# The down product of the second feed-forward as seven block products per chunk

## The chip, the cores and the metric

The kernel runs on one core of one Trainium2 chip. The metric is the device time of one launch in microseconds, the median of the runs shown. One execution of it was also recorded by the hardware profiler. The engines are named as the profile names them: PE multiplies matrices (PEld loads its weights beside it), DVE is the vector engine, ACT the scalar engine, POOL the GpSimd engine, and SP issues the transfers.

## The reference, cut to what matters

The program is a block with a gated linear attention mixer and a feed-forward, and a second block with a hybrid mixer and another feed-forward. The change is in the last stage, the second feed-forward, over 1024 tokens and a model width of 1024, in float32:

```
D_FF = 4 * D_MODEL                                   # 4096
h = rms_norm(x, norm_mlp[l])
x = x + jnp.square(jax.nn.relu(h @ w_up[l])) @ w_down[l]
return rms_norm(x, norm_final)
```

## The kernel before

**Precision.** Every float32 product is made of three matmuls. Each operand is split into a high part (ACT copies it to the shorter type, `Ring.high`) and a low part (POOL subtracts the high part from the whole, `Ring.low`; for activations it is DVE). The three are high by high, high by low, low by high.

**Stage.** `square_ffn` walks over D_FF in 16 chunks of 256 columns. A chunk i has an *up* part (`up(i)`), whose 256 by 1024 result (columns of D_FF by tokens) is made as seven block products named P1, P5, P7, P6, P2, P4, P3 by `PRODUCTS`, in four PSUM banks (tiles PA and PB). Each of the seven has 12 matmuls of 128x512. Sums of the four weight blocks are needed for it, and POOL makes four of them per chunk (`pair_low`, into S, which the profile calls f_sums, and over a block of the raw weights). Before them POOL multiplies the two raw weight tiles by the norm's weights (`weigh`, 128x1024 each). DVE joins the results (`combine`, five adds), ACT applies relu, and DVE multiplies relu by the value (`prod`) for the square.

The *down* part of chunk i takes the activations of up(i-1), 256 by 1024, and the matching 256 rows of w_down. It has 16 output tiles of 128 tokens by 512 columns, in the four PSUM banks of DD and MM in turn, each with 2 times 3 matmuls. DVE adds each tile to X (`add`, 128x512) and raises `down_add`; PE waits for it before it writes a bank again. That is 84 up matmuls and 96 down matmuls in a chunk, and 11 split weight blocks (7 up, 4 down).

**Order.** PE does up(0), and then up(i), down(i) for i = 1 to 15, and then the down part of the last 256 rows (chunk 16) together with the final norm, tile by tile. Everything is written out by hand: each engine runs its own list in order and waits on semaphores. The split weight blocks go through a ring of six slots (`views`, `free`): ACT may write a slot's high part only when PE has used what was there (`used`). `split` counts the low parts that POOL has made, `hi_done` the high parts. SP loads the raw weights: the up tiles of the next chunk when POOL has made all but one of this chunk's low parts (`load_pair`), the down rows into slots of their own (`load_down`), 256 KB each.

**ACT's list in a chunk** (`rest` and the loop): three weight highs, the two activation highs (`a_high`, 128x1024), three weight highs, `keep` (a copy of one bank), one high, four down highs, and relu of both banks.

**DVE's list in a chunk**: `combine`, 16 times `add` with `prod` after the first two, then `a_low` twice (128x1024, both inputs in SBUF). PE waits for `a_lo` only once per chunk, ahead of its first down tile.

## Time and profile before

| | us |
|---|---|
| median of 3 runs | 2822.59 |
| lowest and highest | 2822.29, 2824.02 |
| span of the profiled execution | 2819.2 |

The span is what the profiler saw from the first to the last instruction; it is 3.4 us under the median. The last stage starts on PE at 2154.25 us of the span, and its 15 chunks with an up and a down part follow each other from 2174.99 us on. In the profile, a timeline has one line per instruction with its start and its duration in us; `x2` is two of them merged, and brackets tell how long the engine was idle before it and what ended that. PEclk 1.00 is the full clock of PE.

### The profile page before, as it was taken

The numbers are of one execution on the slowest core, as the hardware profiler recorded it, in microseconds if no ns is written. First come the engines' busy times: TensorE is split into PE (matmuls) and PEld (weight loads), VectorE is DVE, ScalarE is ACT, GpSimd is POOL, SyncE is SP. The second block draws the span as 40 slices with busy tenths as digits, with TensorE's granted clock in tenths as the row PEclk, the third lists the DMA queues.
The fourth block names the chain that finished last, engine by engine and source line by source line (L and its number), as shares of the span: only waits on it lengthen the run. The fifth ranks groups of instructions, "written<-read, shape, count | busy, mean of one in ns | idle before, by whom it ended". The sixth has DMA issues, their size and how long they took to land. (4 is left out here: it accounts for less than half of the span.)

```text
span 2819.2 us, 38148 instructions
## 1 busy us (share of the span) xinstructions
PE 2738.8 (97%) x13551; PEld 2268.4 (80%) x13551; DVE 1538.5 (55%) x1922; ACT 1044.7 (37%) x1516; POOL 1611.9 (57%) x1096
## 2 busy tenths in 40 slices
PE   8999998999999999799999999999999999999998
PEld 7888886888888887678778778778787888888887
DVE  5334435556555556666676666667634444444445
ACT  4312316333333333554355354454424222222223
POOL 3333336767777766865566566466436565565552
PEclk9999999999999999999999999999999999999999
DMA  3111111111111212211121112112420121122112
GB/s 123 46 38 37 45 38 31 43 48 45 59 53 48 63 45 75 82 49 57 38 64 46 50 48 61 44 51 63 164 92 21 55 60 45 44 60 60 41 48 97
DMA packets 200723, 160.27 MB, mean 57 GB/s; under 512 B 6231, under 2 KB 176812, under 8 KB 200621
## 3 DMA queue, kind: packets, MB, share of 16 engines
q1 hardware_dynamic: 200621, 158.83, 18.7%
q8 instruction: 73, 1.20, 0.2%
q14 instruction: 29, 0.24, 0.0%
HBM read 143.08 MB, written 15.73 MB: 56 GB/s over the span
## 5 line engine op out<-in xcount | busy, mean ns | idle before, releaser
L339 POOL TENSOR_TENSOR w_lo<-w_raw,w_hi 128x512 fp32r<-128x512 f32 x272 | 383.0, 1414 | 229.2 <-ACT w_hi L333 229.2
L443 PE MATMUL PA<-h_hi,w_hi 128*128 128x512 f32 x816 | 330.1, 404 | 18.8 <-ACT hy_t L2562 6.1
L445 PE MATMUL PA<-h_hi,w_lo 128*128 128x512 f32 x816 | 319.3, 391 | 0.0
L444 PE MATMUL PA<-h_lo,w_hi 128*128 128x512 f32 x816 | 319.2, 391 | 0.0
L339 POOL TENSOR_TENSOR w_lo<-f_sums,w_hi 128x512 fp32r<-128x512 f32 x114 | 186.2, 1633 | 173.5 <-ACT w_hi L333 173.5
L333 ACT CAST w_hi<-w_raw 128x512 fp32r<-128x512 f32 x272 | 163.9, 616 | 236.4 <-DMA w_raw<-in_w_in 116.6
L443 PE MATMUL PB<-f_t_hi,w_hi 128*128 128x512 f32 x544 | 215.8, 397 | 8.5 <-ACT hy_tm L2621 5.0
L444 PE MATMUL PB<-f_t_lo,w_hi 128*128 128x512 f32 x544 | 213.1, 392 | 0.0
L445 PE MATMUL PB<-f_t_hi,w_lo 128*128 128x512 f32 x544 | 213.0, 392 | 0.0
L339 POOL TENSOR_TENSOR w_lo<-w_lo_raw,w_hi 128x512 fp32r<-128x512 f32 x108 | 139.6, 1299 | 115.9 <-ACT w_hi L333 115.9
L443 PEld LDWEIGHTS PA<-h_hi,w_hi 128*128 128x128 f32 x816 | 154.2, 189 | 55.7 <-issue 14.0
L444 PEld LDWEIGHTS PA<-h_lo,w_hi 128*128 128x128 f32 x816 | 154.1, 189 | 34.0 <-issue 3.8
L445 PEld LDWEIGHTS PA<-h_hi,w_lo 128*128 128x128 f32 x816 | 154.0, 189 | 32.9
L395 POOL TENSOR_TENSOR w_raw<-w_raw,params 128x1024 f32<-128x1024 f32 x72 | 136.4, 1915 | 69.5 <-DMA w_raw<-in_ffn_w_up 45.1
L339 POOL TENSOR_TENSOR w_lo<-hy_ring_sums,w_hi 128x512 fp32r<-128x512 f32 x96 | 139.9, 1457 | 61.2 <-ACT w_hi L333 61.2
L136 PE MATMUL DD<-w_hi,f_a_lo 128*128 128x512 f32 x400 | 155.6, 389 | 0.0
L134 PE MATMUL DD<-w_hi,f_a_hi 128*128 128x512 f32 x400 | 155.6, 389 | 0.0
L135 PE MATMUL DD<-w_lo,f_a_hi 128*128 128x512 f32 x400 | 155.6, 389 | 0.0
L134 PE MATMUL MM<-w_hi,f_a_hi 128*128 128x512 f32 x400 | 155.6, 389 | 0.0
L135 PE MATMUL MM<-w_lo,f_a_hi 128*128 128x512 f32 x400 | 155.6, 389 | 0.0
L136 PE MATMUL MM<-w_hi,f_a_lo 128*128 128x512 f32 x400 | 155.6, 389 | 0.0
L333 ACT CAST w_hi<-f_sums 128x512 fp32r<-128x512 f32 x114 | 70.8, 621 | 204.7 <-PE MM L136 99.9
(561 smaller groups left out, 7119.1 us busy)
## 6 DMA issues: line engine op xcount, KB each, us to landing
w_raw<-in_w_in SPq DMA_DIRECT2D x64, 512.0 KB, 5.2
w_raw<-in_ffn_w_up SPq DMA_DIRECT2D x42, 512.0 KB, 4.7
w_lo_raw<-in_w_down SPq DMA_DIRECT2D x64, 256.0 KB, 2.6
w_raw<-in_w_up SPq DMA_DIRECT2D x30, 512.0 KB, 5.1
w_raw<-in_gla_w_in SPq DMA_DIRECT2D x24, 512.0 KB, 3.8
w_lo_raw<-in_ffn_w_down SPq DMA_DIRECT2D x44, 256.0 KB, 2.6
X<-in_x SPq DMA_DIRECT2D x8, 512.0 KB, 7.2
w_raw<-in_gla_w_out SPq DMA_DIRECT2D x8, 512.0 KB, 3.6
```

Source lines behind the costliest of these rows:

```text
L134: pe.matmul(out, ah, bh, start=first, stop=False)
L135: pe.matmul(out, ah, bl, start=False, stop=False)
L136: return pe.matmul(out, al, bh, start=False, stop=last)
L333: act.copy(self.slot(i, p)[0], source).then_inc(self.hi_done, 1)
L339: pool.tensor_tensor(lo, source, hi.bitcast(F32), ALU.subtract).then_inc(self.split, 1)
L395: pool.tensor_tensor(raw, raw, column.unsqueeze(2).broadcast_to([P, KT, P]), ALU.mult)\
L443: pe.matmul(bank, ah[:, k, :], bh[:, k, :], start=(k == 0 and not more), stop=False, skip_group_check=more)
L444: pe.matmul(bank, ah[:, k, :], bl[:, k, :], start=False, stop=False, skip_group_check=more)
L445: mm = pe.matmul(bank, al[:, k, :], bh[:, k, :], start=False, stop=(k == 3), skip_group_check=more)
```

## The change

The down part of chunks 1 to 15 becomes a seven-product scheme like the up part's. The activations of a chunk are four blocks of 128 by 512 tokens (A11, A21, A12, A22), the rows of w_down four blocks of 128 by 512. Each of the seven products P1, P2, P5, P4, P6, P7, P3 has four tiles of 128 tokens, one in each bank of DD and MM, with three matmuls per tile. P2, P4 and P3 are accumulated on the product that stands in the bank already. After each product DVE reads all four banks, two at a time (`take`, 128x1024), into one quarter of X. So that one quarter is enough, X is held with one quarter subtracted from two others: two subtractions of 128x2048 at the start of the stage and two additions before the last chunk. The last chunk keeps the old form.

Other engines change with it. The split weight blocks are 14 in a chunk, in a ring of seven slots (`TurnRing`, the seventh being f_seventh). POOL makes four sums of the down rows (`row_low`). The down rows are loaded as two 512 KB transfers into the same raw tiles as the up tiles, each when POOL has made the low parts of the blocks that were in it, and the next up tiles when the last two low parts of the down rows are made (`load_up`, `load_rows`). The activation highs and lows are seven per chunk of 128x512, with four sums of activation blocks on DVE (`first_blocks`), all of them with both inputs in SBUF. The square is made by ACT (1024 wide, twice) and no longer by DVE. In `fall`, ACT's highs of the next chunk's up tiles stand between the activation highs P6, P7 and P3. In `combine` the names and signs of the banks are changed, and with them the sign of one block sum in the hybrid stage's norm (`negated`) and of one sum on POOL (`reversed`).

```
 class TurnRing(Ring):
+    UP, DOWN_PRODUCTS = 7, ("P1", "P2", "P5", "P4", "P6", "P7", "P3")
+    def slot(self, i, p):
+        n = self.place(i, p)[0] % 7
+        if n == 6:
+            return self.seventh
...
+    def free(self, i, p):
+        g = self.place(i, p)[1]
+        return 0 if isinstance(g, int) and g < 7 else g - 6
...
+    def load_up(self, sp, i, tiles):
+        for n, p in enumerate((12, 13)):
+            sp.wait_ge(self.split, self.done(i - 1, p))
+            sp.dma_start(self.core.raw[:, n, :].rearrange("p (k n) -> p k n", k=KT), tiles[n])\
+              .then_inc(self.raw_in[n], 16)
+    def load_rows(self, sp, i, sources, behind=None):
+        for n, p in enumerate((4, 5)):
+            sp.wait_ge(self.split, self.done(i if behind is None else behind, p))
+            sp.dma_start(self.core.raw[:, n, :], sources[n]).then_inc(self.raw_in[n], 16)
...
+    def row_low(self, pool, i):
+        first = 4 * (i - 1)
+        (b11, b12), (b21, b22) = [[self.quarter(k, h) for h in range(2)] for k in range(2)]
+        pool.wait_ge(*self.down_arrived(0, i))
+        pool.wait_ge(self.split, self.done(i, 6))
+        pool.tensor_tensor(self.S, b11, b12, ALU.subtract).then_inc(self.mixed, 1)
+        self.low(pool, i, 7, b11)
+        pool.wait_ge(*self.down_arrived(1, i))
+        self.low(pool, i, 8, b21)
+        pool.wait_ge(self.mixed, first + 1)
+        pool.tensor_tensor(b12, b12, b22, ALU.subtract).then_inc(self.mixed, 1)
+        self.low(pool, i, 9, self.S)
+        pool.wait_ge(self.split, self.done(i, 9))
+        pool.tensor_tensor(self.S, b22, self.S, ALU.add).then_inc(self.mixed, 1)
+        pool.wait_ge(self.mixed, first + 3)
+        pool.tensor_tensor(b21, b21, self.S, ALU.subtract).then_inc(self.mixed, 1)
+        self.low(pool, i, 10, b21)
+        self.low(pool, i, 11, self.S)
+        self.low(pool, i, 12, b12)
+        self.low(pool, i, 13, b22)
...
             @block.tensor
+                def down(i):
+                    for n, product_name in enumerate(DOWNS):
+                        more = product_name in ("P2", "P3", "P4")
+                        pe.wait_ge(ring.split, ring.done(i, 7 + n))
+                        pe.wait_ge(s["a_lo"], made(i, MADE.index(product_name) + 1))
...
+                        for b in range(4):
+                            wait(pe, s["down_add"], (i - 1) * 28 + (4 * (n - 1) + b + 2))
+                            tok = slice(b * P, (b + 1) * P)
+                            pe.matmul(bank(b), hi[:, tok], wh, start=not more, stop=False, skip_group_check=more)
+                            pe.matmul(bank(b), hi[:, tok], wl, start=False, stop=False, skip_group_check=more)
+                            mm = pe.matmul(bank(b), lo[:, tok], wh, start=False, stop=True, skip_group_check=more)
...
             @block.scalar
                 def keep(i):
                     act.wait_ge(ring.used, ring.done(i, 0))
+                        act.wait_ge(s["a_sum"], i * 4 - 1)
+                        act.wait_ge(s["a_lo"], made(i, 4))
...
+                def rise(i):
+                    high(i, 6)
+                    a_high(i, "P1", "P2", "P4", "P5")
+                    keep(i)
+                    for n in range(7):
+                        ring.row_high(act, i, n)
+                def fall(i, following):
+                    a_high(i, "P6")
+                    following(0)
+                    a_high(i, "P7")
+                    relu_first(i)
+                    a_high(i, "P3")
+                    following(1)
+                    relu_second(i)
...
             @block.vector
+                def first_blocks(i):
+                    for x in ("P1", "P2", "P4"):
+                        a_low(i, x)
+                    dve.tensor_tensor(A22, A21, A22, ALU.add).then_inc(s["a_sum"], 1)
+                    dve.tensor_tensor(A21, A11, A21, ALU.subtract).then_inc(s["a_sum"], 1)
+                    a_low(i, "P5")
+                    dve.tensor_tensor(A11, A22, A11, ALU.subtract).then_inc(s["a_sum"], 1)
+                    dve.wait_ge(s["a_sum"], i * 4 - 1)
+                    dve.tensor_tensor(A12, A12, A11, ALU.subtract).then_inc(s["a_sum"], 1)
...
+                def take(i, x):
+                    n = DOWNS.index(x)
+                    block_, op = TAKE[x]
+                    for b in range(0, 4, 2):
+                        dve.wait_ge(*((s["down_mm"], (i - 1) * 21 + (3 * n + 2)) if b == 0 else
+                                      (ring.used, ring.done(i, 7 + n))))
+                        rows_ = block_[:, b:b + 2, :]
+                        two = (c.DD, c.MM)[b // 2].rearrange("p (b n) -> p b n", b=2)
+                        dve.tensor_tensor(rows_, rows_, two, op).then_inc(s["down_add"], 2)
...
```

The diff is cut to what the prediction speaks of (blank lines inside it too).

DVE in the last chunk with an up part (i = 15), before, from the first down tile on. Each row is an instruction with its line, its output and inputs and its shape; f_u is U, the activations:

```order
L2092 TENSOR_TENSOR X<-X,DD 128x512
L2077 TENSOR_TENSOR f_u_12892<-f_u_12892,PA 128x1024
L2092 TENSOR_TENSOR X<-X,DD 128x512
L2077 TENSOR_TENSOR f_u_12893<-f_u_12893,PB 128x1024
L2092 TENSOR_TENSOR X<-X,MM 128x512 x2
L2092 TENSOR_TENSOR X<-X,DD 128x512 x2
```

The same place in the changed kernel, in its chunk 1, from the first down product on (f_a_lo is a low part of an activation block):

```order
L2257 TENSOR_TENSOR X<-X,DD 128x2x512
L2257 TENSOR_TENSOR X<-X,MM 128x2x512
L2257 TENSOR_TENSOR X<-X,DD 128x2x512
L2257 TENSOR_TENSOR X<-X,MM 128x2x512
L2220 TENSOR_TENSOR f_a_lo_12900<-f_u_12894,f_a_hi_12896 128x512
L2257 TENSOR_TENSOR X<-X,DD 128x2x512
L2257 TENSOR_TENSOR X<-X,MM 128x2x512
L2220 TENSOR_TENSOR f_a_lo_12901<-f_u_12894,f_a_hi_12897 128x512
L2257 TENSOR_TENSOR X<-X,DD 128x2x512
L2257 TENSOR_TENSOR X<-X,MM 128x2x512
L2220 TENSOR_TENSOR f_a_lo_12903<-f_u_12895,f_a_hi_12899 128x512
```

Three low parts now stand between the reads of PSUM, and each read takes two banks.

ACT at the end of the changed kernel's part for chunk 15 (`fall`): f_a_hi_12896, 12897 and 12899 are the activation highs P6, P7 and P3. In the loop the weight highs between them are those of the next chunk's up tiles, here those of the last down rows:

```order
L2164 CAST f_a_hi_12896<-f_u_12894 128x512
L334 CAST w_hi<-w_raw 128x512
L2164 CAST f_a_hi_12897<-f_u_12894 128x512
L2136 ACTIVATE f_u_12894<-PA 128x1024
L2138 ACTIVATE f_u_12894<-f_u_12894 128x1024
L2164 CAST f_a_hi_12899<-f_u_12895 128x512
L334 CAST w_hi<-w_raw 128x512
```

Before, ACT's two activation highs stood together, with no weight high between them:

```order
L2011 CAST f_a_hi_12894<-f_u_12892 128x1024
L2011 CAST f_a_hi_12895<-f_u_12893 128x1024
L1999 COPY f_u_12892<-PA 128x512
...
L333 CAST w_hi<-f_sums 128x512
...
L333 CAST w_hi<-w_lo_raw 128x512
```

So a weight high that waits now holds up the activation highs behind it.

## Rows read from the trace of the kernel before

**Rows 1.** The page: share of the span, then granted clock in 40 slices.
```profile
PE 2738.8 (97%) x13551; PEld 2268.4 (80%) x13551; DVE 1538.5 (55%) x1922; ACT 1044.7 (37%) x1516; POOL 1611.9 (57%) x1096
...
PEclk9999999999999999999999999999999999999999
```

**Rows 2.** Busy time in one chunk: start:end us, sum, each engine, clock, DMA share, GB/s.
```profile
2231.60:2272.40 40.80, 40.80 (x181) 33.78 (x181) 18.85 (x25) 10.86 (x16) 23.75 (x18) 1.00 0.18 51
```

**Rows 3.** Timeline of PE at a chunk's first down tile (start, us, engine, line).
```profile
2275.64 0.39 PE L134 MATMUL DD<-w_hi,f_a_hi 128*128 128x512 f32 x1
...
2276.77 0.39 PE L136 MATMUL DD<-w_hi,f_a_lo 128*128 128x512 f32 x1
```

**Rows 4.** Timeline of DVE in the same chunk.
```profile
2277.20 0.69 DVE L2092 TENSOR_TENSOR X<-X,DD 128x512 f32<-128x512 f32 x1 [0.66 <-PE DD L136]
2277.80 1.21 DVE L2077 TENSOR_TENSOR f_u<-f_u,PA 128x1024 f32<-128x1024 f32 x1
2278.93 0.68 DVE L2092 TENSOR_TENSOR X<-X,DD 128x512 f32<-128x512 f32 x1
...
2298.75 2.36 DVE L2058 TENSOR_TENSOR f_a_lo<-f_u,f_a_hi 128x1024 fp32r<-128x1024 f32 x2 [0.47 <-ACT f_a_hi L2011]
```

**Rows 5.** Timeline of PE where it waits for DVE before the last chunk.
```profile
2786.77 0.39 PE L136 MATMUL MM<-w_hi,f_a_lo 128*128 128x512 f32 x1
2788.03 0.47 PE L134 MATMUL DD<-w_hi,h_hi 128*128 128x512 f32 x1 [0.87 <-DVE X L2092]
2788.33 0.40 PE L135 MATMUL DD<-w_lo,h_hi 128*128 128x512 f32 x1
```

**Rows 6.** Timeline of DVE around that wait.
```profile
2787.19 0.69 DVE L2092 TENSOR_TENSOR X<-X,MM 128x512 f32<-128x512 f32 x1 [0.67 <-PE MM L136]
```

**Rows 7.** Timeline of DVE at the start of the stage.
```profile
2180.46 1.69 DVE L2058 TENSOR_TENSOR f_a_lo<-f_u,f_a_hi 128x1024 fp32r<-128x1024 f32 x1
2183.40 1.23 DVE L2058 TENSOR_TENSOR f_a_lo<-f_u,f_a_hi 128x1024 fp32r<-128x1024 f32 x1 [1.25 <-POOL w_lo L339]
```

**Rows 8.** Timeline of POOL in the same stretch, and at the stage's first low part P6.
```profile
2159.33 1.29 POOL L339 TENSOR_TENSOR w_lo<-f_sums,w_hi 128x512 fp32r<-128x512 f32 x1
...
2179.78 3.52 POOL L339 TENSOR_TENSOR w_lo<-f_second_raw,w_hi 128x512 fp32r<-128x512 f32 x2
2183.49 2.29 POOL L339 TENSOR_TENSOR w_lo<-f_sums,w_hi 128x512 fp32r<-128x512 f32 x1 [0.19 <-ACT w_hi L333]
```

**Rows 9.** Line of a DVE product of two 512-wide SBUF inputs: ns min/median/max.
```profile
L2844 DVE TENSOR_TENSOR hy_k<-hy_k,hy_f x48: 678/689/1793, 1247.1 to 2043.4; 128x512 f32<-128x512 f32 x48
```

**Rows 10.** Timeline of ACT: highs of 512, relu of 1024.
```profile
2155.55 0.62 ACT L333 CAST w_hi<-w_raw 128x512 fp32r<-128x512 f32 x1 [0.72 <-POOL w_raw L417]
...
2177.01 1.02 ACT L2004 ACTIVATE f_u<-DD 128x1024 f32<-128x1024 f32 x1
```

**Rows 11.** Timeline of POOL in one chunk.
```profile
2236.30 3.76 POOL L395 TENSOR_TENSOR w_raw<-w_raw,params 128x1024 f32<-128x1024 f32 x2 [1.83 <-DMA w_raw<-in_w_up]
2240.24 1.30 POOL L408 TENSOR_TENSOR f_sums<-w_raw 128x512 f32<-128x512 f32 x1 [0.18 <-POOL w_raw L395]
2241.49 1.30 POOL L339 TENSOR_TENSOR w_lo<-w_raw,w_hi 128x512 fp32r<-128x512 f32 x1
...
2246.62 1.30 POOL L339 TENSOR_TENSOR w_lo<-f_sums,w_hi 128x512 fp32r<-128x512 f32 x1 [2.58 <-ACT w_hi L333]
2247.99 1.29 POOL L420 TENSOR_TENSOR f_sums<-f_sums,w_raw 128x512 f32<-128x512 f32 x1
```

**Rows 12.** Timeline of SP: the next chunk's up tiles are issued.
```profile
2232.00 1.02 SPq L351 DMA_DIRECT2D w_raw<-in_w_up  x2
```

**Rows 13.** Timeline of PE: the stage's first matmuls.
```profile
2154.25 0.47 PE L443 MATMUL DD<-h_hi,w_hi 128*128 128x512 f32 x1 [3.01 <-PEq L930]
...
2155.45 0.63 PE L444 MATMUL DD<-h_lo,w_hi 128*128 128x512 f32 x1
```

**Rows 14.** Timeline of PE: the first matmul of chunk 1.
```profile
2174.99 0.39 PE L443 MATMUL PA<-h_hi,w_hi 128*128 128x512 f32 x1
```

More of the change, by code:

```diff
@@ L1936, in chunk @@
                         ring.pair_low(pool, i, 0, i, part)
-                    for h in range(2):
-                        down(i, h)
+                    ring.row_low(pool, i)
                 chunk(1)
@@ L1942, in _ @@
                     chunk(i)
-                for h in range(2):
-                    down(chunks, h)
+                for p in range(4):
+                    ring.last_row_low(pool, chunks, p)
             @block.tensor
@@ L1962, in tile, with last_tile @@
+                def last_tile(m, h, n):
+                    pe.wait_ge(s["down_add"], adds + n - 2)
                     for k in range(2):
[L1963 to L1975 removed]
@@ L1977, in _ @@
-                up(0)
-                chunk(1)
-                with pe.Fori(2, chunks) as i:
-                    chunk(i)
-                pe.wait_ge(s["a_lo"], chunks * 2)
+                        mm = product(pe, bank(n), (last_hi[k][:, m * P:(m + 1) * P], last_lo[k][:, m * P:(m + 1) * P]),
+                                     ring.slot(chunks, 2 * h + k), k == 0, k == 1)
+                    return mm
+                up(0)
+                up(1)
+                pe.wait_ge(s["relu"], 3)
@@ L2042, in _ @@
+                fall(chunks - 1, lambda n: n < 4 and ring.last_row_high(act, chunks, n))
                 last_high(0)
                 last_high(1)
-                for h in range(2):
-                    for k in range(2):
-                        down_high(chunks, h, k)
                 tail.scalar(act)
@@ L2112, in last @@
+                with dve.Fori(2, chunks) as i:
+                    chunk(i)
+                for k in range(2):
+                    dve.wait_ge(s["a_hi"], made(chunks, k + 1))
+                    dve.tensor_tensor(last_lo[k], U[k], last_hi[k].bitcast(F32), ALU.subtract).then_inc(s["a_lo"], 1)
+                dve.wait_ge(s["down_add"], adds + 1)
+                dve.tensor_tensor(X12, X12, X22, ALU.add)
+                dve.tensor_tensor(X21, X21, X22, ALU.add)
+                dve.drain()
                 def last(m):
```

328 lines of the change are left out of this document (191 added, 137 removed).

## The prediction

> **What bounds the kernel now.** I first read the page: PE is busy for 97% of the span at the full granted clock [rows 1]. Then I cut the last stage into its chunks: in each, PE is busy for all of the 40.80 us, DVE for 18.85, ACT for 10.86 and POOL for 23.75 [rows 2]. A busy PE need not be at its peak, so I looked at its timeline: one down tile has six matmuls, and the sixth starts 1.13 us after the first [rows 3], 0.2267 us each. A chunk's 180 matmuls at this pace are 40.80 us, the whole chunk. So PE alone sets the stage, and the others have 17 us and more of slack each. The question is whether they keep it.
>
> **PE's own work.** Down falls from 96 matmuls to 7 x 4 x 3 = 84, a chunk from 180 to 168. 168 x 0.2267 = 38.08 us: 2.72 us less in each of 15 chunks, 40.8 us in all, if nothing waits.
>
> **The hand-over of banks.** Before, PE writes a bank again four tiles of 1.36 us later, and DVE needs 0.69 us for a tile [rows 4]. Now a tile has three matmuls (0.68 us), a product four tiles (2.72 us), and DVE reads two banks in one instruction. Count from a product's first matmul. The last matmul of the second bank starts at 5 x 0.2267 = 1.13. DVE starts 0.43 after such a start (2276.77 to 2277.20) [rows 3, 4]: 1.56. A 1024-wide instruction with one input in PSUM takes 1.21 [rows 4], to 2.78. PE starts a matmul 0.15 after DVE's end (2787.19 + 0.69 = 2787.88, then 2788.03), and the matmul after it comes 0.30 later and not 0.23, 0.08 lost with the next [rows 5, 6]. The next product thus starts at 2.93 and counts as 3.01, not 2.72. Six of the seven products wait like this (the first finds banks long read): 6 x 0.28 = 1.7 us per chunk. This is without any other work on DVE.
>
> **The blocks between.** After the reads of P2, P5 and P4 DVE makes a low part of 128x512. Two reads at 1.13 apart [rows 4] and 0.60 for the low part are 2.86 us, just over what a product gives. Both inputs of the low part are in SBUF, and such instructions take turns with POOL's. At 2179.78 POOL has two low parts, 3.52 us for what is 2.54 alone, and between them stands DVE's L2058 from 2180.46, 1.69 us for about 1.2; at 2183.49 a POOL instruction that starts 0.09 after DVE's takes 2.29 instead of 1.29 [rows 7, 8]. Whichever comes second waits out the whole instruction of the other. The 512-wide form takes 0.69 alone and up to 1.79 [rows 9]: its own 0.6 and up to 1.2 of waiting. DVE now has 11 of them per chunk (7 lows, 4 sums), where it had two 1024-wide.
> The Trainium skill ("SBUF — State Buffer", Who interferes with whom) says the same as a rule: a DVE instruction with two SBUF inputs and a GpSimd one that reads SBUF exclude each other, and issue order decides who blocks. It adds that DVE with at most one SBUF input, as in the reads of PSUM, is free of it; the trace agrees as far as `add` shows, 0.69 us though POOL is weighing at that place of a chunk [rows 4, 11].
>
> **POOL's own line.** 14 lows, 4 sums of up blocks and 4 of down blocks, 1.25 apart (2240.24, 2241.49), and two weighings in 3.76 [rows 11]: 22 x 1.25 + 3.76 = 31.3 us. Where an instruction waits for the one ahead, 0.08 more (2246.62 + 1.30 to 2247.99) [rows 11], six times: 0.5. The next up tile can be loaded only after low 13 of 14, and its first weighing starts 4.30 us after the issue (2232.00 to 2236.30) [rows 11, 12]; only one low, 1.25, covers it: 3.1 us idle. One high part must be waited for in `row_low` (the block just summed): 0.03 + 0.62 + 0.04 [rows 10], 0.7. That is 35.6 us, and up to 11 x 0.6 = 6.6 more where DVE's instructions fall into POOL's: 42.2 at most, above PE's 38.1. So POOL's 17 us of slack are gone.
>
> **What costs nothing.** The 16 adds become 14 reads, 14 x 1.13 = 15.8 for 16 x 0.60; with 11 x 0.60 and the five of `combine` DVE has about 25 us of work in a chunk. The square moves from DVE (2 x 1.21) to ACT, which with 21 highs of 0.53, 4 us of relu and square and a copy has 16 us. Both are covered by PE's 38; if they were not, each would cost its excess. What costs is where they wait. The down rows come as two 512 KB transfers for four of 256 KB; POOL has two lows (2.5 us) between issue and use, and up to 1.8 us more of idle time if they land as late as the up tiles, which the 4.4 us below swallow.
>
> **One chunk walked through.** With these durations (ACT's highs 0.62 and 0.53 apart, 1024 wide 1.03 [rows 10]), from the first up matmul of a chunk, in steady state. 0.2: ACT makes the last up high, whose slot is free only when the chunk before has ended. 0.7 to 1.8: highs of activation blocks P1, P2, P4. DVE's lows of them run into POOL's line, 0.6 + 1.2 + 1.2 of waiting, and with two sums the high of P5 starts at 6.9. `keep` waits for the third sum, 8.8. Only behind it come the highs of the down rows, 9.3, so POOL, ready at 5.6, makes its first down low at 10.0: 4.4 us idle. From there its line runs on: low 13 of 14 ends at 22.2, the load lands, weighing ends at 28.5. ACT's next entry, the next chunk's first high, waited for that; behind it stands the activation high P7 at 29.2. DVE waits for it with the reads of P4 behind, and against POOL: low P7 from 29.8 to 31.1. PE's P6 starts at 32.3 instead of 31.1. The low of P3 behind ACT's relu and square waits in the same way (33.8, to 35.3), and P7 starts 1.3 us late again. The chunk ends at 42.4: 38.1 + 1.7 + 1.3 + 1.2 + 0.1. A chunk is 1.6 us longer than before.
>
> **Ends of the stage.** Chunk 1: the activation highs lie where the second pair of raw up tiles was, so ACT may start them only after POOL's low of P4, which at 40.8 per chunk was no matter. POOL gets there 8.2 us into the chunk, high P1 starts at 9.5, and `keep` comes at 16.3, where PE wanted P2 at 10.9. That is 6 us of waiting and with the later ones 9 us over the old chunk. Start: the two subtractions of 128x2048, some 2.3 us each by the 1024-wide row's pace, take turns with POOL, whose low P6 had been done at 2160.6, about 2 us before PE came to it [rows 8]; PE starts the stage at the lower clock level (0.63 us a matmul at 2155.45, full pace later) [rows 13], which helps to cover: +2, between 0 and 4. Last chunk: PE waits for two 1024-wide lows that stand behind the last two reads, 1.6 + 2 x 1.14 + the hand-over, against the 0.87 us it waited before [rows 5]: +3, while the final additions of 4.5 us hide under four tiles.
>
> **The sum.** Chunk 1 began at 2174.99 [rows 14]. Thirteen chunks (2 to 14) x 1.6 = 21, chunk 1 +9, start +2, last chunk +3: +35 us. The profiled span would be 2854, and the median, 3.4 above it, 2822.6 + 35 = 2858.
>
> **Bounds.** Landing of the up tiles at 3.0 instead of 4.3 gives 42.0 per chunk and about +30; DVE's or POOL's instructions 0.05 to 0.1 longer beside each other give 43.1 to 43.3 and +46 to +48. If POOL's lock costs only POOL or only DVE, the chunk is between 40.3 and 41.8: +3 to +22.
>
> **Rivals.**
> 1. *The turn-taking costs nothing here*, since the 512-wide instructions slip between POOL's. Then the hand-overs and ACT's order remain: 38.1 + 1.7 + 0.5 = 40.3 per chunk, -0.5 x 13 = -7, chunk 1 +6, end +2: 2824. For it speaks that many of POOL's instructions in the trace are undisturbed; against it rows 7 to 9, and that POOL will be busy for over three quarters of a chunk. The Trainium skill's rule, in the same section, would forbid it.
> 2. *PE gets its full 2.72 us*, with DVE keeping pace because reads and hand-over overlap better than I count: -41 us to -20, 2782 to 2802, the side on which the kernel is faster. One number decides it: from the start of the second bank's last matmul to the time PE wants the first bank again there are 2.72 - 1.13 = 1.59 us, and the rows give 0.43 + 1.21 + 0.15 = 1.79.
> 3. *Waits feed on each other*: ACT's registers and semaphores cost more in its longer list, and PE's clock falls after the waits of chunk 1 as it stands at the lower level at 2155 after 3.01 us idle [rows 13]. At 43.5 to 44 per chunk: +50 to +60, 2873 to 2883.
> 4. *The change does not do what it says*: excluded but for detail, since 84 down matmuls and 14 two-bank reads per chunk stand in the code.
>
> **Chances.** Forecast with its bounds (2838 to 2872) 0.64; rival 3 0.10; a cheaper lock, between the forecast and rival 1 (2826 to 2838) 0.08; rival 1 0.12, of which half within 0.2%, the rest on either side; rival 2 0.06. A measurement of this kernel tells about 0.2%, 5.6 us, from no change. Slower by more than that: 0.64 + 0.10 + 0.07 + 0.03 = 0.84; within it 0.07; faster 0.09. The range reaches from 2826, above rival 1, to 2877, in the middle of rival 3.
>
> **What would show it.** Right: PE's idle time in the stage becomes 4 us per chunk, put down to DVE's reads (L2257); chunk period near 42.4; DVE's L2220 over 0.69 us on the mean and POOL's lows over 1.29; ACT's high after the weighing directly ahead of the activation high P7; 6 us before P2 in chunk 1. Wrong: periods under 40.8, which would mean the reads are no hand-over cost; a period at 40.3 with stalls of 0.2 to 0.3 only at each product would be rival 1; a clock under 1.00 in the stage would be rival 3.

## The result, and the profile after

| | us |
|---|---|
| before, median of 4 runs | 2823.06 (2822.29 to 2824.02) |
| after, median of 4 runs | 2861.11 (2859.56 to 2866.77) |
| ratio, with its 95% interval | 1.0139 (1.0125 to 1.0154) |
| span of the profiled execution of after | 2865.0 |

The changed kernel is 38 us slower, 1.4%. The forecast was 2858. The profiled execution of after is the longest of its four (the other spans are 2857.8 to 2859.7): its last stage begins 5.7 us later than in the profile of before (2159.96 for 2154.25 [rows 13]), ahead of all that was changed.

The page's first part, busy time, share of the span and instructions of each engine:

```profile
PE 2735.8 (95%) x13371; PEld 2233.2 (78%) x13371; DVE 1733.9 (61%) x1999; ACT 1129.8 (39%) x1684; POOL 1756.7 (61%) x1201
```

PE is at 95% for 97% [rows 1]. The stretch view of the last stage, one chunk, then the sum and mean of six (PE, PEld, DVE, ACT, POOL busy with their instructions, the granted clock, DMA share, GB/s):

```profile
2426.52:2469.27 42.75, 40.05 (x170) 30.99 (x169) 31.53 (x31) 16.37 (x27) 33.22 (x25) 1.00 0.16 49
...
sum 255.50, PE 239.93 PEld 185.45 DVE 187.83 ACT 98.22 POOL 198.40; mean PE 39.99 PEld 30.91 DVE 31.30 ACT 16.37 POOL 33.07
```

A chunk is 42.6 us (twelve periods from 2256.28 to 2767.74 by the issues of the up tiles), where it was 40.80 [rows 2]. PE has fewer matmuls, DVE has 31.3 us of work for 18.85, POOL 33.1 for 23.75. Matmuls of one chunk in PE's timeline (start, duration, line, tiles, in brackets the idle time and what ended it):

```profile
2471.60 0.50 PE L2091 MATMUL DD<-w_hi,f_a_hi 128*128 128x512 f32 x1
2471.94 0.40 PE L2092 MATMUL DD<-w_lo,f_a_hi 128*128 128x512 f32 x1
...
2474.69 0.50 PE L2091 MATMUL DD<-w_hi,f_a_hi 128*128 128x512 f32 x1
...
2479.36 0.50 PE L2091 MATMUL DD<-w_hi,f_a_hi 128*128 128x512 f32 x1 [1.64 <-DVE X L2257]
...
2483.55 0.50 PE L2091 MATMUL DD<-w_hi,f_a_hi 128*128 128x512 f32 x1 [1.18 <-DVE X L2257]
```

Each L2091 row here is the first matmul of a down product (P5, P4, P6, P7). P4 begins 3.09 us after P5, which is the hand-over: predicted 3.01 with no other work on DVE. P6 begins 4.67 after P4 and P7 4.19 after P6, for 2.72 of matmuls (on the mean of chunks 3 to 14: 4.41 and 4.20). These two waits stand where the forecast put them, behind the activation highs P7 and P3. ACT, POOL and DVE at the same place:

```profile
2475.44 0.62 ACT L334 CAST w_hi<-w_raw 128x512 fp32r<-128x512 f32 x1 [6.25 <-POOL w_raw L396]
2475.96 0.62 ACT L2164 CAST f_a_hi<-f_u 128x512 fp32r<-128x512 f32 x1
```

```profile
2473.43 1.90 POOL L396 TENSOR_TENSOR w_raw<-w_raw,params 128x1024 f32<-128x1024 f32 x1 [3.07 <-DMA w_raw<-in_w_up]
2475.72 1.90 POOL L396 TENSOR_TENSOR w_raw<-w_raw,params 128x1024 f32<-128x1024 f32 x1 [0.39 <-DMA w_raw<-in_w_up]
2477.80 1.50 POOL L409 TENSOR_TENSOR f_sums<-w_raw 128x512 f32<-128x512 f32 x1 [0.18 <-POOL w_raw L396]
```

```profile
2474.76 1.22 DVE L2257 TENSOR_TENSOR X<-X,MM 128x1024 f32<-128x1024 f32 x1
2476.61 1.55 DVE L2220 TENSOR_TENSOR f_a_lo<-f_u,f_a_hi 128x512 fp32r<-128x512 f32 x1 [0.63 <-ACT f_a_hi L2164]
2478.09 1.21 DVE L2257 TENSOR_TENSOR X<-X,DD 128x1024 f32<-128x1024 f32 x1
...
2480.86 1.50 DVE L2220 TENSOR_TENSOR f_a_lo<-f_u,f_a_hi 128x512 fp32r<-128x512 f32 x1 [0.43 <-ACT f_a_hi L2164]
```

ACT sits 6.25 us in front of the next chunk's first weight high, which waits for POOL's weighing (L396, which itself waited 3.07 for the transfer). The activation high P7 (L2164) comes directly behind it. DVE stood ready for 0.63, and its low part then takes 1.55 us where it takes 0.69 alone, because POOL's second weighing runs until 2477.6; only then can it read P4's banks (2478.09). The groups of DVE, and then of POOL, in thirteen periods (times, busy us, mean ns of one, idle time before and what ended it):

```profile
L2257 DVE TENSOR_TENSOR X<-X,DD 128x1024 f32<-128x1024 f32 x92 | 111.9, 1217 | 31.4 <-PE DD L2093 31.4
L2220 DVE TENSOR_TENSOR f_a_lo<-f_u,f_a_hi 128x512 fp32r<-128x512 f32 x91 | 101.8, 1141 | 14.6 <-ACT f_a_hi L2164 14.6
L2241 DVE TENSOR_TENSOR f_u<-f_u,f_u 128x512 f32<-128x512 f32 x13 | 22.0, 1689 | 0.0
```

```profile
L340 POOL TENSOR_TENSOR w_lo<-w_raw,w_hi 128x512 fp32r<-128x512 f32 x104 | 134.2, 1301 | 64.3 <-ACT w_hi L334 64.3
...
L396 POOL TENSOR_TENSOR w_raw<-w_raw,params 128x1024 f32<-128x1024 f32 x26 | 51.2, 1974 | 41.0 <-DMA w_raw<-in_w_up 40.6
L340 POOL TENSOR_TENSOR f_seventh_lo<-f_sums,f_seventh_hi 128x512 fp32r<-128x512 f32 x13 | 22.6, 1739 | 0.0
```

The low part's mean is 1141 ns for about 690 alone, L2241's 1689. On POOL, a low part that is 1290 alone is 1739 at one place of the chunk. The reads L2257, one input in PSUM, stay at 1217 [rows 4].

### The profile page after: what moved, and what is told of

Its sections match the earlier page's. It is cut to its first block and busy times, and to the rows that moved or that the text cites. A ratio compares the mean times of both kernels' runs of the same rounds, so it can differ in the third digit from the quotient of the medians.

```text
span 2865.0 us, 39045 instructions
## 1 busy us (share of the span) xinstructions
PE 2735.8 (95%) x13371; PEld 2233.2 (78%) x13371; DVE 1733.9 (61%) x1999; ACT 1129.8 (39%) x1684; POOL 1756.7 (61%) x1201
## 5 line engine op out<-in xcount | busy, mean ns | idle before, releaser
L340 POOL TENSOR_TENSOR w_lo<-w_raw,w_hi 128x512 fp32r<-128x512 f32 x336 | 462.0, 1382 | 319.4 <-ACT w_hi L334 319.4
L546 PE MATMUL PA<-h_hi,w_hi 128*128 128x512 f32 x636 | 262.1, 412 | 17.7 <-ACT hy_t L2739 6.4
L547 PE MATMUL PA<-h_lo,w_hi 128*128 128x512 f32 x636 | 251.2, 395 | 0.0
L548 PE MATMUL PA<-h_hi,w_lo 128*128 128x512 f32 x636 | 251.1, 395 | 0.0
L396 POOL TENSOR_TENSOR w_raw<-w_raw,params 128x1024 f32<-128x1024 f32 x72 | 138.9, 1944 | 87.5 <-DMA w_raw<-in_w_up 43.8
L546 PE MATMUL PB<-f_t_hi,w_hi 128*128 128x512 f32 x424 | 169.3, 399 | 9.9 <-ACT hy_tm L2798 5.0
L2257 DVE TENSOR_TENSOR X<-X,DD 128x1024 f32<-128x1024 f32 x105 | 127.7, 1217 | 35.4 <-PE DD L2093 35.4
L548 PEld LDWEIGHTS PA<-h_hi,w_lo 128*128 128x128 f32 x636 | 121.6, 191 | 26.3
L2257 DVE TENSOR_TENSOR X<-X,MM 128x1024 f32<-128x1024 f32 x105 | 127.8, 1217 | 10.5 <-PE MM L2093 3.8
L2220 DVE TENSOR_TENSOR f_a_lo<-f_u,f_a_hi 128x512 fp32r<-128x512 f32 x105 | 115.7, 1124 | 25.9 <-ACT f_a_hi L2164 25.9
L334 ACT CAST w_hi<-hy_ring_sums 128x512 fp32r<-128x512 f32 x96 | 59.6, 621 | 138.2 <-POOL hy_ring_sums L409 67.1
L2091 PE MATMUL DD<-w_hi,f_a_hi 128*128 128x512 f32 x180 | 78.6, 436 | 37.1 <-DVE X L2257 34.4
```

The source lines that it names most:

```text
L334: act.copy(self.slot(i, p)[0], source).then_inc(self.hi_done, 1)
L340: pool.tensor_tensor(lo, source, hi.bitcast(F32), ALU.subtract).then_inc(self.split, 1)
L396: pool.tensor_tensor(raw, raw, column.unsqueeze(2).broadcast_to([P, KT, P]), ALU.mult)\
L546: pe.matmul(bank, ah[:, k, :], bh[:, k, :], start=(k == 0 and not more), stop=False, skip_group_check=more)
L547: pe.matmul(bank, ah[:, k, :], bl[:, k, :], start=False, stop=False, skip_group_check=more)
L548: mm = pe.matmul(bank, al[:, k, :], bh[:, k, :], start=False, stop=(k == 3), skip_group_check=more)
```

## The experiments

All are the changed kernel with the edits that are shown or named. lows_psum, all_psum, all_psum_tiny and all_psum_single read some operands from a PSUM bank that holds something else, and tiny_reads and all_psum_tiny leave most of the reads out, so the results of these five are not the reference's; every instruction is still there. "Chunk" is the mean period of the up tiles' issues from the fourth on (eleven periods), in the profiled execution; the times are medians. Where an experiment gives a time inside a chunk, it is the mean of chunks 3 to 14 in the profiled execution, counted from the chunk's first up matmul.

| run | time, us | ratio to before (95%) | chunk, us |
|---|---|---|---|
| after | 2861.11 | 1.0139 (1.0125, 1.0154) | 42.62 |
| lows_psum | 2847.63 | 1.0083 (1.0066, 1.0100) | 41.47 |
| all_psum | 2833.49 | 1.0036 (1.0022, 1.0050) | 40.46 |
| single | 2860.63 | 1.0126 (1.0110, 1.0143) | 42.54 |
| tiny_reads | 2854.94 | 1.0113 (1.0096, 1.0130) | 42.48 |
| all_psum_tiny | 2796.66 | 0.9905 (0.9886, 0.9924) | 38.27 |
| all_psum_single | 2803.39 | 0.9931 (0.9913, 0.9949) | 38.58 |
| p7_first | 2861.31 | 1.0136 (1.0118, 1.0155) | 42.49 |
| order_single | 2829.78 | 1.0023 (1.0013, 1.0033) | 40.37 |
| squares_only | 2844.63 | 1.0068 (1.0053, 1.0084) | 41.35 |
| squares_single | 2800.22 | 0.9918 (0.9905, 0.9932) | 38.31 |
| squares_found | 2804.02 | 0.9930 (0.9916, 0.9943) | 38.79 |
| squares_two | 2847.42 | 1.0080 (1.0063, 1.0097) | 41.68 |

My theory: a chunk is set by a ring of waits, each of which releases the next until the last one lets the next chunk begin. They are: activation highs, DVE's lows and sums in turns with POOL, `keep`, down highs, POOL's lows, the load, the weighing, ACT's next entry, the activation high and low P7, PE's P6. Rival: the hand-over of banks is the cause, and the rest only fills it.

### Is it the turn-taking? (lows_psum, all_psum)

The edits, with the ends of lines (`.then_inc`) left out here and below:

```
-    dve.tensor_tensor(alo[k], BLOCK[x], ahi[k].bitcast(F32), ALU.subtract)
+    block_ = up_banks(i)[3] if x in ("P6", "P7", "P3") else BLOCK[x]    # lows_psum
+    block_ = up_banks(i)[3] if x in ("P6", "P7", "P3") else bank(0)     # all_psum
+    dve.tensor_tensor(alo[k], block_, ahi[k].bitcast(F32), ALU.subtract)
-    dve.tensor_tensor(A22, A21, A22, ALU.add)                           # all_psum, and the
+    dve.tensor_tensor(A22, bank(0), A22, ALU.add)                       # other three sums
```

> The low parts of P6, P7 and P3, which stand between the reads on DVE, take their first input from a free PSUM bank and not from the activations (their values are then not the reference's). DVE's count of instructions, order and waits stay; only two inputs in SBUF become one. Theory (turn-taking with POOL makes P6 and P7 late): each of the three takes 0.69 us and no more, POOL has no long instruction beside them, the chunk falls from 42.6 to about 41.2 us, and the time by 20 us to 2841. Rival A (the hand-over of banks is what costs, and the low parts only happen to lie there): 0.60 of work is still between the reads, no change, 2858 to 2864. Rival B (ACT's order behind POOL's weighing costs alone): P7 still waits, at most 0.3 per chunk less, 2856 or more.

> All eleven 512-wide instructions of DVE that had two inputs in SBUF (seven low parts, four sums) take one of them from a free PSUM bank (their values are then not the reference's). Theory: besides the gain above, POOL's line loses up to eight further waits for DVE, the down lows begin earlier, the next up tile lands earlier, and the weighing ends before ACT's list comes to it: chunk about 40.3 to 40.5 us, -32 us, 2829. What remains over 38.1 are hand-overs and ACT's order. Rival A (hand-over): 2858 to 2864. Rival C (only the three low parts between the reads matter, those at a chunk's start have slack): the same as the run with three, 2841.

Measured: -13.5 us, less than the 20 expected, and -27.6 us for 32; chunks of 41.47 and 40.46, for 41.2 and 40.3 to 40.5. In lows_psum DVE's groups split into those with both inputs in SBUF and those with one in PSUM (PB):

```profile
L2221 DVE TENSOR_TENSOR f_a_lo<-f_u,f_a_hi 128x512 fp32r<-128x512 f32 x52 | 59.8, 1189 | 2.0 <-ACT f_a_hi L2164 1.9
L2221 DVE TENSOR_TENSOR f_a_lo<-PB,f_a_hi 128x512 fp32r<-128x512 f32 x39 | 26.9, 689 | 15.7 <-ACT f_a_hi L2164 15.7
```

Same operation, same size, same neighbours: 1189 against 689 ns. PE's two waits fall from 1.64 and 1.18 to:

```profile
2468.91 0.50 PE L2091 MATMUL DD<-w_hi,f_a_hi 128*128 128x512 f32 x1 [1.16 <-DVE X L2258]
...
2472.29 0.50 PE L2091 MATMUL DD<-w_hi,f_a_hi 128*128 128x512 f32 x1 [0.36 <-DVE X L2258]
```

In all_psum POOL's low part is back at its own time, and PE's whole list of waits is this (us in total, times, longest), where after has 31.4 us in 25 times for DVE over as many chunks, and 1.2 for POOL:

```profile
L340 POOL TENSOR_TENSOR f_seventh_lo<-f_sums,f_seventh_hi 128x512 fp32r<-128x512 f32 x13 | 17.0, 1309 | 0.0
```

```profile
PE DD L2091 <- DVE X L2258: 4.0, 12, 0.3
```

So the turn-taking is shown as a cause, and rivals A and C fall: the eight instructions at a chunk's start, which PE never waits for directly, give as much again as the three between the reads. The way it reaches PE shows between lows_psum and all_psum: `keep` comes at 6.0 us into the chunk for 9.2, the next up tiles are issued at 19.8 for 23.0, the activation high P7 is made at 26.3 for 29.6, and what P6 is late over 2.72 us falls from 1.28 to 0.34.

### Is it the hand-over? (single, tiny_reads)

```
-    for b in range(0, 4, 2):
+    for b in range(4):                                       # single
...
-        dve.tensor_tensor(rows_, rows_, two, op).then_inc(s["down_add"], 2)
+        dve.tensor_tensor(rows_, rows_, bank(b), op).then_inc(s["down_add"], 1)
```

tiny_reads keeps the two-bank form with `[:, b:b + 2, 0:4]` and `two[:, :, 0:4]`.

> DVE reads the down banks one at a time: four 128x512 reads for a product, each released by its own bank, for two of 128x1024. Theory: the hand-over wait of 0.28 us goes at the products where DVE has no low part between (P2's, P7's, P3's), but the time goes into longer waits for P6 and P7, whose low parts come no earlier, since the chain over POOL's weighing and ACT sets them: chunk 42.3 to 42.5, -5 us, 2856 (DVE also gets 28 x 0.60 = 16.8 us of reads for 15.8). Rival A (hand-over is what costs): -1.7 us per chunk, -24 us, 2837. Rival D (DVE is too full): longer than 2861.

> DVE's fourteen reads per chunk stay with their waits and signals but cover 4 of 512 columns of each bank, so X is nearly left out (about 0.1 us each for 1.21). Theory: all hand-over waits go (1.7 us per chunk), but P6 and P7 wait for their low parts longer, since their highs come behind POOL's weighing: chunk about 42.3, -6.5 us, 2854. Rival A (hand-over is what costs): chunk 40.5 or less, 2835 or less, and DVE's freed 15 us let the low parts come as they are wanted.

Measured: single -0.5 us, tiny_reads -6.2 us (expected -6.5). Their chunks are 42.54 and 42.48. Taking 14 us of DVE's work out of a chunk (31.3 to 17.2), and every hand-over wait with it, shortens the chunk by 0.14 us. That is under 2 us of the 6.2: in the profiled executions chunk 1 and chunk 15 are 2.4 us shorter each (48.74 for 51.13, 42.00 for 44.36), outside the chunks that the expectation spoke of, so its time was met in part by luck. Within a chunk `keep` comes 1.3 us later than in after (10.15 for 8.86) and P6 starts at 32.6 for 32.5: PE gets through its first down products sooner and then waits for the same ring. PE's waits of tiny_reads in thirteen periods:

```profile
PE DD L2091 <- DVE X L2257: 36.0, 18, 3.1
```

After has 31.4 us in 25 times there: fewer now, but longer, 2.0 us on the mean for 1.3, and 3.1 at most. So by itself the hand-over costs almost nothing here; rival A falls. In both runs something came that I had not expected. The first row is P6 of single; the later ones come 0.43 apart, not 0.23:

```profile
2477.78 0.50 PE L2091 MATMUL DD<-w_hi,f_a_hi 128*128 128x512 f32 x1 [2.60 <-DVE X L2256]
...
2479.65 0.63 PE L2091 MATMUL MM<-w_hi,f_a_hi 128*128 128x512 f32 x1
2480.08 0.63 PE L2092 MATMUL MM<-w_lo,f_a_hi 128*128 128x512 f32 x1
```

Two neighbouring chunks of single, the first at a mean granted clock of 0.96:

```profile
2383.46:2426.02 42.56, 39.83 (x168) 32.45 (x168) 32.64 (x45) 16.37 (x27) 32.83 (x25) 0.96 0.16 49
2426.02:2468.58 42.56, 38.85 (x170) 31.50 (x169) 32.73 (x45) 16.31 (x27) 32.97 (x25) 1.00 0.16 49
```

Both take 42.56. In the first PE waits 2.73 us before P6 and not at all before P7; in the second it waits 2.51 and then 1.20 again. So the lost clock costs nothing here, as it only fills time that the ring would have taken. That fits a chunk that PE's pace does not set. As expected, the waits for P6 and P7 grew as the others went: P6 is 2.76 late for 1.69, P7 1.60 for 1.48. Why the time of single fell by 0.5 us and not by the 5 expected is open; the stage of its profiled execution is 3.3 shorter than that of after (701.8 for 705.0), and single came out 1.6 longer behind chunk 15.

### Do the two cover each other? (all_psum_tiny, all_psum_single)

The edits of all_psum together with that of tiny_reads, and together with that of single.

> The eleven instructions with one input in PSUM, as before, and the reads cut to 4 of 512 columns (both values are then not the reference's). Theory: the two causes cover each other, so that the reads alone gave 6 us and the turn-taking alone 28, but both together give more than the sum: no hand-over waits and no late low parts, PE at its floor of 168 x 0.2267 = 38.1 us per chunk, -65 us, 2796. Rival A (the gains add): 28 + 6 = 34, 2827, a chunk of 40.3. Rival E (something else bounds the chunk, POOL's line of 35.6 us with the landing of the up tiles, or ACT): between, 39 to 40 us per chunk, 2808 to 2822.

> The eleven instructions with one input in PSUM and the reads one bank at a time, 28 of 0.69 us. Theory: without turn-taking the hand-over is what is left, and now one-bank reads pay: chunk 38.7 to 38.9 us, -56 us, 2805. So the two-bank read costs 1.6 to 1.8 us per chunk here (against all_psum at 40.46), where it cost nearly nothing (42.62 against 42.54) with the turn-taking. Rival (the two-bank read is never worth anything, or DVE is too full with 28 reads): 40.3 or more, 2830.

Measured: 2796.66 and 2803.39, against 2796 and 2805. A chunk of all_psum_tiny, PE busy in all of it:

```profile
2477.60:2515.68 38.08, 38.08 (x169) 31.46 (x168) 12.63 (x30) 16.58 (x27) 31.66 (x25) 1.00 0.18 55
```

That is PE's floor, 168 x 0.2267 = 38.1; the mean of the chunks is 38.27. Alone the two edits gave 28 and 6 us, together 64. With the turn-taking out of the way the two-bank read costs 40.46 - 38.58 = 1.9 us per chunk against one-bank reads; with it in place, 0.1. Rivals A and E fall, and POOL's line with its load does not bound the chunk at 38.3.

### Is it ACT's order? (p7_first)

```
     a_high(i, "P6")
-    following(0)
     a_high(i, "P7")
+    following(0)
     relu_first(i)
```

> ACT makes the activation high P7 ahead of the next chunk's first weight high, which waits for POOL's weighing; nothing else is moved. Theory: P7's high no longer waits for the weighing, its low part falls to where its operand slot is free, PE's wait for P6 shrinks, but P7 still waits for the low of P3 behind relu and square, and the weight high is 0.5 to 1 us later, which POOL feels at the chunk's start: 42.1 to 42.3 us per chunk, -6 us, 2855. Rival F (ACT's order is the cause by itself and the turn-taking only fills the wait): 41.4 or less, -17 us or more, 2844. Rival G (no matter at all, DVE's low is late by the reads of P5 ahead of it): 2861.

Measured: 2861.31, no gain: a miss. The chunk went from 42.62 to 42.49. DVE no longer waits for the high, but look at its low part (1.97) and at POOL at the same time:

```profile
2470.05 1.22 DVE L2259 TENSOR_TENSOR X<-X,MM 128x1024 f32<-128x1024 f32 x1
2471.18 1.97 DVE L2222 TENSOR_TENSOR f_a_lo<-f_u,f_a_hi 128x512 fp32r<-128x512 f32 x1
2473.07 1.21 DVE L2259 TENSOR_TENSOR X<-X,DD 128x1024 f32<-128x1024 f32 x1
```

```profile
2470.70 1.90 POOL L396 TENSOR_TENSOR w_raw<-w_raw,params 128x1024 f32<-128x1024 f32 x1 [0.15 <-DMA w_raw<-in_w_up]
```

The low part, at once behind the reads, now meets the second weighing nearly from its start, waits it out, and ends at 2473.15, 3.10 us after the start of the last read ahead of it, where after has 3.40 (2474.76 to 2478.16). Most of the 0.63 of waiting for ACT became turn-taking: the low part starts 0.66 earlier and lasts 1.88 for 1.35. The time is that of rival G, and its reason, the reads of P5 ahead of the low part, is half of it: the low part starts directly behind them, but then waits for POOL as well. So ACT's order alone gives next to nothing back, though the forecast's walk had booked 1.3 us per chunk beside it.

### Whole kernels: other orders, and squares in PSUM (order_single, squares_only, squares_single, squares_found, squares_two)

order_single: ACT's list at the fall and DVE's list, written short. At the rise the activation highs P1, P2, P4 and P5 now stand ahead of weight high 6, and the reads are of one bank:

```
+    a_high(i, "P6"); a_high(i, "P7"); following(0); a_high(i, "P3"); relu_first(i)
+    following(1); relu_second(i)
...
+    take P1, take P2, a_low P6, a_low P7, take P5, take P4, a_low P3, take P6, P7, P3
```

> A whole kernel with nothing left out and other orders. ACT at the fall of a chunk: activation highs P6, P7, weight high 0, activation high P3, relu and square of the first pair, weight high 1, and so on; at the rise the activation highs P1, P2, P4, P5 ahead of weight high 6. DVE: low parts of P6 and P7 both behind the reads of P2, the low of P3 behind the reads of P4; reads one bank at a time. Theory: each low part is made one product earlier than PE wants it, so neither the turn-taking nor ACT's order shows on PE: chunk 40.4 to 40.6 us, -32 us, 2829. That would still be no faster than the kernel before (2823), since first chunk, start and end keep their 12 us. Rival A (hand-over): half of it, 2845. Rival H (the turn-taking itself, not the order, takes the time): 42 or more, 2855.

Measured 2829.78, 40.37 per chunk, as expected. The expectation held that neither cause would show on PE any more; PE still waits:

```profile
PE PA L2073 <- ACT f_u L2129: 14.0, 12, 1.2
PE DD L2091 <- DVE X L2258: 5.0, 11, 1.2
```

P2 of the up part waits for `keep` (L2129), 1.2 us each chunk: `keep` comes behind DVE's lows and sums at a chunk's start, which take turns with POOL in any order. So the next edit takes operands out of SBUF there. ACT squares into the down banks, idle at that time:

```
-    act.activation(U[0], U[0], ACT.Square).then_inc(s["sq"], 1)      # in relu_first
-    act.activation(U[1], U[1], ACT.Square).then_inc(s["sq"], 1)      # in relu_second
+    act.wait_ge(s["down_add"], (i - 1) * 28 + 1)                     # squares, now in rise(i)
+    act.activation(bank(0), A11, ACT.Square).then_inc(s["sq"], 1)
+    act.activation(A21, A21, ACT.Square)
+    act.activation(c.MM, U[1], ACT.Square).then_inc(s["sq"], 1)
...
-    dve.tensor_tensor(A22, A21, A22, ALU.add)
+    dve.tensor_tensor(A22, A21, bank(3), ALU.add)                    # and so on
```

> A whole kernel, nothing left out. ACT takes the squares not at the fall, in place, but at the rise of the next chunk, and writes three of the four blocks to the down banks, which stand empty while PE makes the up part (one block stays in SBUF, since an instruction takes one operand from PSUM). So DVE's lows of P1, P2, P4 and its four sums have one input in PSUM: seven of eleven take no turns with POOL. The three lows between the reads and that of P5 still do. Orders and two-bank reads as in the changed kernel. Theory: keep comes earlier and with it the down rows, the load of the next up tiles and the weighing: chunk 41.2 us, -20 to -23 us, 2838 to 2841. Rival C (only the three lows between the reads matter, which this leaves alone): 2858 or more, and the gain of the run with all eleven over that with three had another source.

> The squares as above, with the orders of order_single (ACT's and DVE's) and reads of one bank at a time; nothing left out. Theory: low parts are never wanted by PE before they are there, and the hand-over is gone: chunk 38.5 to 38.9 us, PE's floor being 38.1, against 40.37 of order_single, and the time 2801 to 2807, about 0.7% faster than the kernel before. Rival I (the remaining four turns, or ACT's squares behind the last reads, keep PE waiting): 39.5 to 40.4 per chunk, 2815 to 2829. Rival A (hand-over alone bounds order_single): no gain over 2829.

> As squares_single, with DVE's low P6 behind the reads of P1, low P7 behind P2's, low P3 behind P6's, and ACT's weight highs 0 and 1 ahead of the activation high P3, 2 and 3 ahead of relu of the second pair, two down highs ahead of keep. Theory: worked out with the row times, 38.1 to 39.6 us per chunk, the wide span since the high P6 must then be there when P1's reads end, and since the landing of the up tiles decides (4.7 us gives the lower, 4.3 the upper end): 2790 to 2815, forecast 2797. Rival J (weight highs before P3's high wait for POOL and hold up relu): 40 or more, 2825.

Measured 2844.63, 2800.22 and 2804.02. squares_only gains 16.5 us (20 to 23 expected), but not for the reason expected: `keep`, which now has the squares ahead of it on ACT, comes at 8.8 us, where it came in after (8.9), and the next up tiles are issued at 22.5 for 22.6. What changed is P7, late by 0.32 us for 1.48. ACT makes the activation high P3 directly behind relu, with no square between:

```profile
2466.75 1.02 ACT L2139 ACTIVATE f_u<-PA 128x1024 f32<-128x1024 f32 x1 [1.19 <-DVE f_a_lo L2239]
2467.67 0.61 ACT L2176 CAST f_a_hi<-f_u 128x512 fp32r<-128x512 f32 x1
```

```profile
2468.90 0.75 DVE L2239 TENSOR_TENSOR f_a_lo<-f_u,f_a_hi 128x512 fp32r<-128x512 f32 x1
```

The high starts at 32.1 us for 33.4, and the low part P3, which still has both inputs in SBUF, meets only the end of one of POOL's instructions and takes 0.75 for 1.50. So this run moved the squares and the operands at once, its gain came mostly from the first, and it says nothing on rival C, which all_psum alone decides. squares_single is 0.8% faster than the kernel before, with all of the work in it. One of its chunks, and the remaining lows with both inputs in SBUF:

```profile
2442.95:2481.30 38.35, 38.35 (x170) 31.38 (x169) 27.84 (x45) 16.26 (x28) 31.95 (x25) 1.00 0.17 55
```

```profile
L2241 DVE TENSOR_TENSOR f_a_lo<-f_u,f_a_hi 128x512 fp32r<-128x512 f32 x52 | 36.3, 719 | 2.1 <-ACT f_a_hi L2176 2.1
...
L2241 DVE TENSOR_TENSOR f_a_lo<-DD,f_a_hi 128x512 fp32r<-128x512 f32 x13 | 9.0, 691 | 44.2 <-ACT f_a_hi L2176 44.2
```

PE is busy throughout, and the mean of the four lows that could still take turns is 719 ns: they meet POOL's reads hardly any more. The wait for `keep` is gone (at 8.95 for 11.49 in order_single). How much of the gain over order_single is due to the operands in PSUM, and how much to the squares' new place, was not tried apart. squares_found, which the row times put at 38.1 to 39.6, measured 38.79, and its time is 7 us over the forecast of 2797: it is no better than squares_single. Working with row times was good to about half a microsecond per chunk, not to a tenth. The last run puts back the two-bank read alone:

```
-    for b in range(4):
+    for b in range(0, 4, 2):                                  # and the read of both
```

> squares_single with one thing put back: DVE reads two banks at a time (14 reads of 1.21 us for 28 of 0.69). Nothing left out. Theory: with low parts early, the read of two banks is what PE waits for: 0.28 us at six products, 1.7 us per chunk, and where a low part lies behind two reads (2.86 us of DVE for a product of 2.72) a little more: worked out 41.3 us per chunk, 2842. A bare count of hand-overs gives 38.3 + 1.7 = 40.0 and 2825. Rival K (the two-bank read is free once the low parts are early): 38.3, 2800.

Measured 2847.42, 47 us over squares_single, 3.4 us per chunk. First matmuls of P5, P4, P6 and P7 ahead of and behind their waits:

```profile
2463.62 0.50 PE L2094 MATMUL DD<-w_hi,f_a_hi 128*128 128x512 f32 x1
...
2467.35 0.50 PE L2094 MATMUL DD<-w_hi,f_a_hi 128*128 128x512 f32 x1 [0.68 <-DVE X L2278]
...
2470.39 0.50 PE L2094 MATMUL DD<-w_hi,f_a_hi 128*128 128x512 f32 x1
...
2474.44 0.50 PE L2094 MATMUL DD<-w_hi,f_a_hi 128*128 128x512 f32 x1 [1.00 <-DVE X L2278]
```

The steps are 3.73, 3.04 and 4.05. A product that waits for reads alone costs the hand-over, 0.3 over 2.72. One that waits for reads with low parts ahead of them costs 1.0 and 1.3. The 1.3 at P7 is not the read's alone. DVE's low part P3 and POOL at that place:

```profile
2471.63 1.62 DVE L2241 TENSOR_TENSOR f_a_lo<-f_u,f_a_hi 128x512 fp32r<-128x512 f32 x1
```

```profile
2471.41 1.29 POOL L340 TENSOR_TENSOR w_lo<-w_raw,w_hi 128x512 fp32r<-128x512 f32 x1
```

The low part takes 1.57 us on the mean here and 0.76 in squares_single: the two-bank reads moved it to where POOL is reading, so up to 0.8 of the 3.4 us is turn-taking that came back. The bare count, 1.7 per chunk, is half of the 3.4; the expectation of 41.3, which had DVE's work between two hand-overs in it, was 0.4 too low. Rival K, a two-bank read that is free, falls. The same edit was worth 0.5 us in the changed kernel and is worth 47 here. squares_two differs from squares_only in the orders alone, and is no faster (2847.42 for 2844.63): here early low parts paid with one-bank reads and not without them.

## Why the prediction was right, point by point

**The chunk.** 42.4 forecast, 42.61 measured over the thirteen chunks 2 to 14: 23.5 us over the old ones for 21. Between the first matmuls of the products P1 to P3 lie 2.91, 3.04, 3.09, 4.67, 4.19 and 3.03 us, that is 0.19, 0.32, 0.37, 1.95, 1.47 and 0.31 over 2.72. This chunk has one of the longest waits for P6. On the mean of chunks 3 to 14 the excess is 0.18, 0.32, 0.38, 1.69, 1.48 and 0.32, and 0.17 to the next chunk, 4.5 in all for 4.3. Forecast were 0.28 each, and by the walk 1.2 more at P6 (32.3 for 31.1) and 1.3 at P7: 1.48 and 1.58. (The sum under the walk has the two the other way round.) P6 was 0.2 too small and P7 0.1 too large. POOL's weighing ran longer (1974 ns on the mean for 1880).

The points of the walk come out too, which a sum that was right by chance would not give (us into the chunk, mean of chunks 3 to 14): `keep` at 8.9 for 8.8, the first down low at 10.0 for 10.0, the issue of the up tiles at 22.6 for 22.2, the activation high P7 at 29.3 for 29.2, its low part 30.0 to 31.3 for 29.8 to 31.1, P6 at 32.5 for 32.3, the low part P3 34.0 to 35.5 for 33.8 to 35.3. One sign was off: PE's idle time was to be 4 us per chunk and is 2.6 (42.58 less 39.99 busy), because the profile records a matmul as 0.39 to 0.50 us long though they start 0.23 apart, so that most of a hand-over delay of 0.2 to 0.4 us lies under a matmul and not in idle time. POOL's waits for ACT's highs, 4.4 before the down lows and 0.7 in `row_low` by the forecast, are 64.3 us in thirteen chunks, 4.9 each.

**Turn-taking.** The Trainium skill ("SBUF — State Buffer", Who interferes with whom) says that DVE with two SBUF inputs and GpSimd reading SBUF exclude each other and that one SBUF input is free of it. The runs agree both ways: 1189 against 689 ns in one kernel, and 28 us for the eleven instructions.

**Rival 1**, turn-taking free of cost, was priced at 40.3 per chunk. The run that removes it measured 40.46. **Rival 2** was decided by 1.79 us against 1.59; the hand-over takes 3.04 us, not 2.72.

**Chunk 1.** Forecast +9. Measured from its first matmul (2182.84) to the next chunk's (2233.97): 51.13 for 40.81, +10.3. The wait before P2 is 6.27 for 6. What the sum had at nothing and I had left to rival 3 alone is the clock, for behind it stand matmuls 0.43 apart, from the second row here on:

```profile
2200.14 0.79 PE L2073 MATMUL PA<-h_hi,w_hi 128*128 128x512 f32 x1 [6.27 <-ACT f_u L2129]
...
2201.16 0.63 PE L2077 MATMUL PA<-h_hi,w_lo 128*128 128x512 f32 x1
2201.59 0.63 PE L2073 MATMUL PA<-h_hi,w_hi 128*128 128x512 f32 x1
```

Eleven of them, 0.2 each, are 2.2 us. The term was mis-sized by this and by later waits that were smaller.

**Start and end.** Start +2 forecast, +2.1 measured (22.88 us from the stage's first matmul to chunk 1, 20.74 before). The last product: +3 forecast; the wait is 3.65 for 0.87 [rows 5], and the clock falls again:

```profile
2832.20 0.50 PE L134 MATMUL DD<-w_hi,h_hi 128*128 128x512 f32 x1 [3.65 <-DVE h_lo L2279]
...
2833.77 0.63 PE L136 MATMUL DD<-w_hi,h_lo 128*128 128x512 f32 x1
```

Chunk 15 with this wait is 2.5 us longer than before, and the matmuls behind it 1.6: 4.1 together.

**The sum** for the profiled execution: 5.7 ahead of the stage, 2.1, 10.3, 23.5 and 4.1 are 45.7; its span is 45.8 over that of before. The stage itself is 40 for 35. The difference is 2.5 on the thirteen chunks, 1.3 in chunk 1 and 1.1 at the end, and the clock alone lost 2.2 and 1.6 in the last two. All three are on the same side, so the total does not rest on errors that cancel; only the small hand-overs within a chunk do so in part (0.18 to 0.38 for 0.28).

**Where the working was less good than the number.** The forecast added 1.7 for hand-overs, 1.3 for ACT's place and 1.2 for relu along PE's line. The sum was right, but the terms are not what each edit gives back: undoing the first gave 0.1 us per chunk, mending the second 0.1, and the turn-taking, which had no term of its own there, 2.2. The third was not undone by itself; squares_only, which does it and more, gave 1.3. I had the ring before me when I walked the chunk, and then booked it as a sum on PE.

## What to carry to other kernels

Ahead of a change that takes matmuls away, look not at whether the other engines have slack, but at whether their work forms a ring that comes back to PE, and walk it once with durations; then price each edit by the ring's length and not by the wait it removes. Where DVE has two operands in SBUF while POOL streams from SBUF, put one of them in a PSUM bank that is idle at that time, if only for a few microseconds: in lows_psum it took 0.5 us off each instruction, and with the squares moved, early lows and one-bank reads it turned 1.4% slower into 0.8% faster. When an edit does two things, look in the trace which of them paid: squares_only came near its forecast by the other one. A wide PSUM read saves DVE's time (15.8 for 16.8 us per chunk by the spacing of the rows, an estimate) and lengthens what the writer waits; which of the two counts depends on which of them is on the ring.

## What the runs showed of the hardware that I had not expected

- After idle times of 2.60 us (P6 in single), 3.65 us (last product) and 6.27 us (chunk 1) PE's matmuls came 0.43 us apart for a while, the lower of its two clock levels; after 1.64 and 1.18 us in after, they stayed at 0.23. In between it went both ways: single also has waits of 2.51 us (at 2435.28) and 2.81 (at 2733.18) with 0.23 behind them. In single the chunks at a mean clock of 0.96 and of 1.00 are equally long, so a lower clock in a row is no proof that time was lost.
- Work that waits its turn shows as a longer duration, not as idle time: in p7_first a low part of 0.69 stands as 1.97 with no releaser named, so a list of waits alone does not show this cause.
- The down rows, two transfers of 512 KB, landed in 3.7 us (median), where four of 256 KB had taken 2.6 each. The up tiles, 512 KB before and after, took 4.7 for 5.1.
